# Gate tiles multiplied between the items of an attention, a one-pass decay row and unpaired first tiles, in a fp32-exact transformer kernel on one Trainium2 core

## The reference, cut to what matters

```python
h = _rms_norm(x, g_mix)
fq, fk, fv, f_logit, dq, dk, dv, gate_a, gate_b = split(h @ w_in)
log_f = log_sigmoid(f_logit + b_fgate)
y_a = fox_attention(fq, fk, fv, log_f)       # 8 heads of 64; scores + c_q - c_k, c = cumsum(log_f)
y_b = diff_attention(q1, q2, k1, k2, dv, lam)  # 4 heads, two score maps each, v of width 128
y_b = rms_norm(y_b, g_diff_sub) * (1 - lambda_init)
merged = sigmoid(gate_a) * (y_a @ w_branch_a) + sigmoid(gate_b) * (y_b @ w_branch_b)
x = x + merged @ w_out
x = x + cross_attention(rms_norm(x), rms_norm(mem))
x = x + moe(rms_norm(x))                     # 32 experts, top 2
```

## Time and profile before

| what | us |
|---|---|
| median of three runs | 2947.47 |
| the runs' range | 2941.38 to 2956.33 |
| the profiled execution's own time | 2968.1 |
| its span, first to last instruction | 2966.3 |
| gate tiles of the second block, PE | 1885.6 to 1972.9 |
| attention of the second block, PE | 1973.6 to 2141.1 |
| merge starts, PE | 2149.2 |

### The profile page before, as it was taken

One profiled execution on the slowest core, in us unless ns is written; L12 is line 12 of the kernel. 1 busy time (PEld: TensorE's weight loads), 2 busy tenths in 40 slices (PEclk: granted clock), 3 DMA queues, 4 the chain that ended last, 5 costly groups with the idle time before them and its releaser, 6 DMA issues.

```text
span 2966.3 us, 37460 instructions
## 1 busy us (share of the span) xinstructions
PE 2731.7 (92%) x12718; PEld 2092.8 (71%) x12718; DVE 1462.4 (49%) x2107; ACT 897.8 (30%) x1468; POOL 1151.4 (39%) x768
## 2 busy tenths in 40 slices
PE   6989898999989889999999999999899699999995
PEld 4768777887867777777887777776576466666662
DVE  4673664122345854751213343015655577887785
ACT  3322322111024213311110020112202376776774
POOL 3752015666747720046666645440053011112120
PEclk9999899999999998999999999987999799999997
DMA  3213002332322111012333222320023199999995
GB/s 125 64 36 93 8 15 78 99 93 91 92 71 73 55 44 58 1 58 98 93 98 109 92 69 88 100 64 1 1 78 121 42 359 344 393 390 358 386 393 201
DMA packets 78151, 373.33 MB, mean 126 GB/s; under 512 B 11216, under 2 KB 11344, under 8 KB 53328
## 3 DMA queue, kind: packets, MB, share of 16 engines
q1 hardware_dynamic: 71888, 360.23, 34.5%
q0 software_dynamic: 5280, 8.40, 0.9%
q10 hardware_dynamic: 864, 3.15, 0.3%
HBM read 368.06 MB, written 12.58 MB: 128 GB/s over the span
## 4 chain that ended last, share of the span: by engine, by line
PE 83%; DVE 6%; POOL 3%; issue 3%; ACT 2%; DMA 2%; DVEq 0%; ACTq 0%; SPq 0%; POOLq 0%
PE PS L1807 16%; PE PS L1808 15%; PE PS L1809 15%; PE PS L2169 6%; PE PS L2192 4%; PE PS L2259 4%; PE PS L2260 4%; PE PS L2289 3%; PE PS L1932 2%; PE PS L1829 2%; PE PS L2183 2%; PE PS L2269 2%; PE PS L2129 2%; PE PS L1884 1%; PE PS L2247 1%
## 5 line engine op out<-in xcount | busy, mean ns | idle before, releaser
L565 POOL TENSOR_SCALAR whi<-ring 128x1024 fp32r<-128x1024 f32 x260 | 293.3, 1128 | 1210.2 <-PE PS L1809 963.5
L568 POOL TENSOR_TENSOR wlo<-ring,whi 128x1024 fp32r<-128x1024 f32 x260 | 655.6, 2522 | 21.7
L1807 PE MATMUL PS<-xh,whi 128*128 128x512 f32 x1264 | 504.9, 399 | 30.8 <-POOL wlo L568 24.3
L1808 PE MATMUL PS<-xl,whi 128*128 128x512 f32 x1264 | 496.6, 393 | 0.0
L1809 PE MATMUL PS<-xh,wlo 128*128 128x512 f32 x1264 | 496.5, 393 | 0.0
L1566 DVE TENSOR_TENSOR arena_r<-arena,arena_r 128x1024 fp32r<-128x1024 f32 x256 | 301.6, 1220 | 90.6 <-ACT arena_r L958 87.8
L1807 PEld LDWEIGHTS PS<-xh,whi 128*128 128x128 f32 x1264 | 240.3, 190 | 88.8 <-issue 17.2
L958 ACT ACTIVATE arena_r<-arena 128x1024 fp32r<-128x1024 f32 x256 | 255.9, 1050 | 91.2 <-DMA arena<-w_gate 91.0
L1808 PEld LDWEIGHTS PS<-xl,whi 128*128 128x128 f32 x1264 | 240.6, 190 | 52.2 <-issue 2.9
L1809 PEld LDWEIGHTS PS<-xh,wlo 128*128 128x128 f32 x1264 | 240.1, 190 | 50.9
L1807 PE MATMUL PS<-xs,whi 128*128 128x512 f32 x560 | 231.2, 413 | 17.4 <-DVE xs L1241 10.1
(11 more groups left out here) (390 smaller groups left out, 4494.0 us busy)
## 6 DMA issues: line engine op xcount, KB each, us to landing
ring<-ring_w SPq DMA_DIRECT2D x280, 512.0 KB, 3.5
arena<-w_gate SPq DMA_DIRECT2D x64, 1024.0 KB, 7.6
arena<-w_up SPq DMA_DIRECT2D x64, 1024.0 KB, 9.2
arena<-w_down SPq DMA_DIRECT2D x64, 1024.0 KB
arena<-y_dram SPq DMA_DIRECT2D x8, 512.0 KB, 7.2
xT<-xT_in SPq DMA_DIRECT2D x1, 2048.0 KB, 8.4
out<-arena SPq DMA_DIRECT2D x4, 512.0 KB, 2.6
arena<-memT_in SPq DMA_DIRECT2D x1, 1024.0 KB, 7.5
```

Source lines behind the costliest of these rows:

```text
L565: nc.gpsimd.tensor_scalar(whi[:, t % 2, :], ring[:, t % RING, :], 1.0, 0.0, ALU.mult, ALU.add).then_inc(sems["whi"], 1)
L568: nc.gpsimd.tensor_tensor(wlo[:, t % RING, :], ring[:, t % RING, :], whi[:, t % 2, :], ALU.subtract).then_inc(sems["split"], 1)
L1807: mm(out, a[0], b[0], start=start, stop=False)
L1808: mm(out, a[0], b[1], start=False, stop=False)
```

## The change

1. **Gate tiles.** Feats 18 to 33 leave `STEPS2`. Their 16 tiles are cut into 64 parts of two chunks (six matmuls each) that PE multiplies at the end of the attention's steps: two parts for each of the items 0 to 7, one for each of the items 8 to 55, none for 56 to 63. They accumulate in PSUM bank 2, so the scores of this attention have two banks and item k waits for the exponential of item k - 2. ACT copies a finished tile out without the sigmoid, one step later. The 16 sigmoids stand at the merge.
2. **The attention's results.** Since `xh` and `xl` stay in use for the gates, the results of query blocks 0 to 2 are kept in fp32 where the queries were (`fq`, `dq`), and split by ACT (`xh`) and DVE (`xl`) in eight chunks of 384 columns in the steps of items 60 to 63. The last query block is split as before. The merge waits for all eight.
3. **Decay row.** `negc` is rounded to fp32r in rows 0 to 7 with its rest in rows 64 to 71, and the selector has a 1 in both rows, so that a single fp32r matmul adds both parts. The selector is loaded to `gtmp` ahead of feat 16 and rounded by ACT into `tabs` (`selr`), on which the attention waits.
4. **First tiles.** `first_pair` is gone. The first tile alone waits chunk by chunk: 16 matmuls on `xh`, 8 on `xl`; the second is an ordinary tile. In `late_norm` ACT squares each chunk right behind its rounding, and the sum over the squares stands one tile earlier on PE.

```diff
+        def banks(items):
+
+            return 2 if items is BL2 else 3
+
+        def gate_parts(it):
+
+            k = it.get("k", 64) if it else 64
+            n = 2 * k if k < 8 else 8 + k
+            return range(n, n + 2 if k < 8 else n + 1) if k < 56 else range(0)
+
+        def late_chunks(it):
+
+            k = it.get("k", 0) if it else 0
+            return range(2 * (k - 60), 2 * (k - 60) + 2) if k >= 60 else range(0)
+
+        done = slice(0, (QT - 1) * P)
+        y_mix = [(fq if j < 4 else dq)[:, j % 4, done] for j in range(8)]
+        late_mix = [it["t"] for it in BL2 if it and it["kind"] == "mix"][2 * QT - 3]
 ...
                     nc.scalar.activation(xh[:, c, :], xT[:, c, :], ACT.Identity, scale=lcol[:, C_FFN + c:C_FFN + c + 1]
                                          ).then_inc(sems["xh"], 1)
-                for c in range(KO):
                     nc.scalar.activation(sq8[:, c, :], xT[:, c, :], ACT.Square).then_inc(sems["sq"], 1)
 ...
-                    elif i < 34:
-                        tables["set"] = None
-                        ins = nc.scalar.activation(sga[:, i - 18, :], src, ACT.Sigmoid)
 ...
+                elif kind == "selr":
+                    act_e.wait_ge(sems["sel"], 16)
+                    nc.scalar.activation(sel_r, sel, ACT.Identity).then_inc(sems["selr"], 1)
+                elif kind == "merge":
+                    tables["set"] = None
+                    act_e.wait_ge(sems["evac"], nth("evac", l, 34))
+                    for c in range(8):
+                        for part in (c, 8 + c):
+                            ins = nc.scalar.activation(sga[:, part, :], sga[:, part, :], ACT.Sigmoid)
+                        ins.then_inc(sems["sgs"], 1)
 ...
+            def gate_evac(l, n):
+
+                i = 18 + n // 4
+                act_e.wait_ge(sems["tile"], nth("tile", l, tile2_of(i) + 1))
+                nc.scalar.activation(sga[:, i - 18, :], PS[:, 2, :], ACT.Identity).then_inc(sems["evac"], 1)
 
             def attend(l, items):
                 ln_exp_tables()
                 for s in range(len(items) + 5):
+                    if items is BL2:
+                        for n in gate_parts(items[s - 1] if 0 < s <= len(items) else None):
+                            if n % 4 == 3:
+                                gate_evac(l, n)
+                        for c in late_chunks(items[s] if s < len(items) else None):
+                            if c == 0:
+                                act_e.wait_ge(sems["tile"], nth("tile", l, tile2_of(33) + 1))
+                                act_e.wait_ge(sems["pt"], nth("pt", l, late_mix + 1))
+                            nc.scalar.activation(xh[:, c, done], y_mix[c], ACT.Identity).then_inc(sems["yh"], 1)
 ...
-                    nc.vector.tensor_scalar(negc[0:8, :], qg[0:8, 0, :], -1.0, None, ALU.mult).then_inc(sems["nck"], 1)
+                    nc.vector.tensor_scalar(negc_r[0:8, :], qg[0:8, 0, :], -1.0, None, ALU.mult).then_inc(v_ch, 1)
+                    v.wait_ge(v_ch, v_step())
+                    nc.vector.scalar_tensor_tensor(out=negc_r[64:72, :], in0=qg[0:8, 0, :], scalar=-1.0,
+                                                   in1=negc_r[0:8, :], op0=ALU.mult, op1=ALU.subtract
+                                                   ).then_inc(sems["nck"], 1)
 ...
-                        v.wait_ge(sems["evac"], nth("evac", l, 34))
+                        v.wait_ge(sems["sgs"], c + 1)
 ...
+                                y, late = it["y"], it["mixn"] > 2 * QT - 2
                                 if "sub" in it:
 
-                                    nc.vector.tensor_scalar(gtmp[:, 0:T], PS[:, 3 + t % 2, :], par[:, M_SUB:M_SUB + 1],
-                                                            0.8, ALU.mult, ALU.mult).then_inc(v_ch, 1)
+                                    ins = nc.vector.tensor_scalar(y, src, par[:, M_SUB:M_SUB + 1], 0.8, ALU.mult,
+                                                                  ALU.mult)
+                                    if late:
+                                        ins.then_inc(v_ch, 1)
+                                        v.wait_ge(v_ch, v_step())
+                                elif late:
+                                    y = src
+                                else:
+                                    ins = nc.vector.tensor_copy(y, src)
+                                if late:
+                                    yh, yl = (x[:, it["dst"], it["cols"]] for x in (xh, xl))
+                                    nc.vector.tensor_copy(yh, y).then_inc(v_ch, 1)
                                     v.wait_ge(v_ch, v_step())
-                                    src = gtmp[:, 0:T].rearrange("p (a b) -> p a b", b=P)
-                                nc.vector.tensor_copy(yh, src).then_inc(v_ch, 1)
-                                v.wait_ge(v_ch, v_step())
-                                ins = nc.vector.tensor_tensor(yl, src, yh, ALU.subtract)
+                                    ins = nc.vector.tensor_tensor(yl, y, yh, ALU.subtract)
 ...
+                    for c in late_chunks(items[s]) if items is BL2 and s < len(items) else ():
+                        v.wait_ge(sems["yh"], c + 1)
+                        nc.vector.tensor_tensor(xl[:, c, done], y_mix[c], xh[:, c, done], ALU.subtract
+                                                ).then_inc(sems["yl"], 1)
 ...
-            def feature_major(out, t):
-
+            def feature_major(l, out, t, wait, wait_low=None):
+
+                if wait is None:
+                    for c in range(KO):
+                        ins = mm3(out, weights(t, slice(c * P, c * P + P)), (xh[:, c, :], xl[:, c, :]),
+                                  start=(c == 0), stop=(c == 7))
+                    return ins
                 for c in range(KO):
-                    ins = mm3(out, weights(t, slice(c * P, c * P + P)), (xh[:, c, :], xl[:, c, :]),
-                              start=(c == 0), stop=(c == 7))
+                    pe.wait_ge(sems["xh"], nth("xh", l, wait + c + 1))
+                    for w in weights(t, slice(c * P, c * P + P)):
+                        mm(out, w, xh[:, c, :], start=(c == 0 and w.name == whi.name), stop=False)
+                for c in range(KO):
+                    pe.wait_ge(sems["xn"], nth("xn", l, (wait if wait_low is None else wait_low) + c + 1))
+                    ins = mm(out, whi[:, t % 2, c * P:c * P + P], xl[:, c, :], start=False, stop=(c == 7))
                 return ins
-
-            def first_pair(l, bank, t, high, low):
-
-                for j in range(2):
-                    pe.wait_ge(sems["split"], nth("split", l, t + j + 1))
-                for c in range(KO):
-                    pe.wait_ge(sems["xh"], nth("xh", l, high + max(c, 1) + 1))
-                    for j in range(2):
-                        for w in weights(t + j, slice(c * P, c * P + P)):
-                            mm(PS[:, bank + j, :], w, xh[:, c, :], start=(c == 0 and w.name == whi.name), stop=False)
-                for c in range(KO):
-                    pe.wait_ge(sems["xn"], nth("xn", l, low + c + 1))
-                    for j in range(2):
-                        ins = mm(PS[:, bank + j, :], whi[:, (t + j) % 2, c * P:c * P + P], xl[:, c, :],
-                                 start=False, stop=(c == 7))
-                        if c == 7:
-                            ins.then_inc(sems["tile"], 1)
 ...
-                    first_pair(l, 0, T_FFI, 8, 8)
-                    for u in range(2, 4):
+                    for u in range(4):
                         pe.wait_ge(sems["split"], nth("split", l, T_FFI + u + 1))
-                        feature_major(PS[:, u, :], T_FFI + u).then_inc(sems["tile"], 1)
-                        if u == 2:
+                        feature_major(l, PS[:, u, :], T_FFI + u, 8 if u == 0 else None).then_inc(sems["tile"], 1)
+                        if u == 1:
 ...
-                elif kind == "feat" and i in (0, 34):
-                    pe.wait_ge(sems["evac"], nth("evac", l, i))
-                    first_pair(l, 0, tile2_of(i), *((0, 0) if i == 0 else (8, 16)))
-                elif kind == "feat" and i not in (1, 35):
+                elif kind == "feat":
 ...
-                        ins = feature_major(PS[:, i % 2, :], t)
+                        ins = feature_major(l, PS[:, i % 2, :], t, {0: 0, 34: 8}.get(i), {0: 0, 34: 16}.get(i))
+                    pe.wait_ge(sems["selr"], 1)
+                    pe.wait_ge(sems["yl"], 8)
 ...
+                        nb = banks(items)
+                        if k >= nb:
+                            pe.wait_ge(sems["p"], nth("p", l, k - nb + 1))
 ...
+                    for n in gate_parts(items[s]) if items is BL2 and s < len(items) else ():
+                        gate_part(l, n)
+
+            def gate_part(l, n):
+
+                i, q = 18 + n // 4, n % 4
+                t = tile2_of(i)
+                if q == 0:
```

(12 more changed lines are left out.)

39 lines of the change are left out of this document (18 added, 21 removed).

## The result

| | before | changed |
|---|---|---|
| first comparison, median of 5 runs each | 2947.47 us (2936.41 to 2956.33) | 2920.32 us (2913.41 to 2922.6) |
| ratio, 95% interval | | 0.9887 (0.985 to 0.9923) |
| a second comparison of the same two kernels | 2952.36 us (17 runs) | 2911.16 us (6 runs), ratio 0.9851 (0.9824 to 0.9878) |
| profiled execution | 2968.1 us, span 2966.3 | 2913.41 us, span 2911.6 |

So the change makes the kernel faster, by 27 us in the one comparison and 41 in the other. 2890 was forecast, with 2872 to 2925 as its range. The second comparison comes from the experiments, where the changed kernel ran once more as after_again.

The account below looks back on a forecast made before the run. TensorE was taken to bound the attention, at half clock in its first part, and GpSimd's splits behind norms. Terms -27 - 14 - 2.5 + 5.5 = -38, with -20 for first tiles -58, from median 2947.47 to 2890 us; range 2872 to 2925.

Parts of the forecast that it names:

- 1, the clock, -27: Second block's attention: gate parts between items keep TensorE's clock up through the half-speed stretch, -27 us, bounds 30 and about 10.
- The dip at the start: Start of the attention: one short clock dip while TensorE waits there, counted as 3 us lost.
- The first rival (clock low in part): Attention: the clock stays low in part, so its gain is 10 us or less; 2915 us, chance 0.13.
- the slower one (gate parts run cold): Attention: gate parts do not lift the clock and run at half speed; +18, 2966 us, chance 0.04.
- 2, decay rows, -14: Attention: decay rows in one fp32r pass instead of fp32, -14 us, bounds 16 and 10.5.
- The sign "0.23 to 0.3 us": Attention: a decay row of 512 columns was to take 0.23 to 0.3 us after the change.
- 3 and 4, gaps and costs of the interleaving, +3 together: Attention: gate parts fill TensorE's waits behind combines, -2.5 us; start, junctions and late splits cost +5.5.
- The item on splits: Gate tiles: GpSimd's splits, 3.5 us each, are hidden behind 5.4 us of gate work plus the items.
- The rival of the binding chain: Attention: with two banks TensorE waits for maximum and exponential in narrow items; 2905 us, chance 0.04.
- 5, first tiles, -20: Behind norms: first tiles run alone, so TensorE no longer waits for GpSimd's third-tile split; -20 us, bounds -6 and -26.
- the forecast for the cross attention's pair (+1): Cross attention's start needs both tiles and no third, so unpairing them costs +1 us.
- the second rival: Behind norms: a thin first tile keeps the clock down through the second; first tiles give -4, 2906 us, chance 0.10.

Follow-up runs that it names:

- gates_alone: Kernel before with only gate parts between the attention's items, sigmoids at the merge and two score banks; 2931.41 us, ratio 0.9925.
- fill experiments: Changed kernel plus 37, 15 or 24 dummy multiplications in the cross attention, results unread; 2911.39, 2909.55 and 2909.45 us.
- no_decay: Changed kernel with its decay rows in fp32 again, as before; 2924.95 us, ratio 0.9905.
- shift: Changed kernel with its gate parts two items earlier, so GpSimd's next split no longer falls beside a combine; 2897.37 us, ratio 0.979.
- pairs_back: Changed kernel with the first tiles behind norms paired again; 2936.62 us, ratio 0.9937.
- first_tiles_alone: Kernel before with only the first tiles behind norms unpaired; 2944.56 us, ratio 0.9971.
- before_again: Kernel before, unchanged, run and profiled again; 2952.6 us, ratio 1.0, span 2948.7.
- after: Changed kernel as first measured and profiled, against the kernel before; 2920.32 us, ratio 0.9887.
- decay_only: Kernel before with only the one-pass decay rows; 2978.73 us, ratio 1.0089.
- before: The kernel without the change, as first measured and profiled; 2947.47 us.
- shift_again: Changed kernel with gate parts two items earlier, the same version run once more; 2906.84 us, ratio 0.985.
- fill_burst: Changed kernel plus 24 dummy multiplications in the first three steps of the cross attention; 2909.45 us, ratio 0.9826.
- fill_light: Changed kernel plus 15 dummy multiplications, 4 behind the cross attention's first step and one behind each of the next 11; 2909.55 us, ratio 0.9822.

## Why the prediction was right, and where not

The direction and the range held (2920.32 and 2911.16, in 2872 to 2925), and the mechanism of the main term too. The likeliest value, 2890, is 21 to 30 us too low, and the gain that it stood for, 58 us, came to 27 and 41. By its steps:

- **1, the clock, -27.** Right. The granted clock is 1.00 through the whole attention, in both traces of the change and also where only this part was made (gates_alone). The dip at the start, for which 3 us were counted, did not come, although TensorE waited 2.00 us there. The first rival (clock low in part) did not happen, and the slower one (gate parts run cold) neither. All ten traces with gate parts in this attention have it at 0.97 or more, with 13.7 us at half clock at most; all four without them have 27 to 150 us of it. That dense multiplications are what holds the clock fits this and the fill experiments, which tried it in another stage. Two score banks did not cost the clock: 1.00 over the attention with two, 0.80 with three before.
- **2, decay rows, -14.** Mis-sized: -9.6 by no_decay against the change. A 512-column row is followed at 2036.74 - 2036.40 = 0.34 us, not 0.23; the narrow ones at 0.17 (128 columns), 0.22 and 0.29, where 0.1 had been taken for the narrow sizes. With these numbers the step's own sum is 8 x (0.62 + 0.46 + 0.32 + 0.16) = 12.5. Another 1.9 us went into waits: with the lighter rows TensorE stands idle for 3.7 us in this attention, with the fp32 rows for 1.8. The last 1.0 us to 9.6 is left unexplained. The sign "0.23 to 0.3 us" for a row of 512 columns was missed with 0.34. The change's rows:

```profile
2036.40 0.50 PE L2215 MATMUL PS<-ekb_r,tabs_r 128*128 128x512 f32 x1
2036.74 0.23 PE L2215 MATMUL PS<-maskb 128*128 128x128 bf16 x1
```

- **3 and 4, gaps and costs of the interleaving, +3 together.** For attention and gates -36.4 was measured and -38 forecast, but this agreement is partly luck. The interleaving (items 1, 3 and 4, forecast -24) gave -28.0 in the trace of gates_alone (226.4 us from the end of the key and value tile to the last product, against 254.4), and the decay rows gave 8.4 where 14 was forecast (9.6 less a wait at the start that grew by 1.2 us with their selector). The two errors have opposite signs. Gaps were to give 2.5; instead, the waits for VectorE behind combines are 3.2 + 0.4 us. The item on splits said "Hidden", and asked only whether TensorE waits for them. It did not ask what GpSimd's work does to VectorE's beside it: that is 4 us (shift). The rival of the binding chain did not come: no wait of TensorE in this attention ended with an exponential. The Trainium skill (SBUF — State Buffer, Who interferes with whom) has this rule: GpSimd and a VectorE operation with two inputs in SBUF take turns at one port, whoever comes second waits for the other to end. The trace agrees, with 2.68 us instead of 0.69.
- **5, first tiles, -20.** Right in sum. Up to the attention the parts were -7.9, -7.2 and -4.4, together -19.5, where its items give -7.6, -10.2 and -5; the saving is 17.2 by pairs_back and 17.6 by first_tiles_alone. TensorE no longer waits for GpSimd there; the forecast for the cross attention's pair (+1) was right too (+1.6 from norm to start). That a first tile with few multiplications leaves the second cold was the second rival; it did not come.
- **The sum, -58.** Up to the cross attention -56.2. The step that failed is the one that ended the list there: it took everything behind the changed stages as unchanged, and wrote "+1" for the cross attention's start and nothing for the stage itself. This stage runs the same kind of short fp32 matmuls whose clock the first item was about, and it ran at half clock in both traces of the change: +14.5.
- **The range.** Its ends have two slips: the upper takes 9 us for item 5, whose own bound was 6 (2928 then), and 2947.5 - 74 is 2873.5, not 2872. Neither matters for the result.
- **The median.** Subtracting from the median instead of the profiled time was right, but the reason offered for the 21 us (a shorter stretch at half clock in the timed runs) was wrong: the profiled execution had two waits for a gather, 16.3 us. With what was measured the sum is 2947.5 - 56.2 + 14.5 + 3.4 (the end of the kernel against before_again) = 2909, against medians of 2920.32 and 2911.16.

The parts do not add up. Alone, against 2952 to 2955: gates -21, first tiles -10, decay rows +24; together -27 to -41. The decay rows are the clearest: with the gates they win 9.6 us, without them they lose 24. Whether the other stages of small matmuls run at half clock decides as much as the work that is removed.

**What stays open:** what decides the level of the cross attention. It was cold in after, after_again, first_tiles_alone, no_decay, decay_only and pairs_back, warm in before, before_again, gates_alone, shift and shift_again. Pairing, decay rows and gates each stand on both sides, so none of them decides it alone. Among the versions with unshifted gate parts and no dummies, those with unpaired first tiles or one-pass decay rows were cold and those with neither warm; only shift, which has both, breaks this. What the traces also show is when the stage starts, counted from the start of the last short dip of the clock ahead of it: 12.2 us in before, before_again and gates_alone (warm) and 12.4 in decay_only and pairs_back (cold), 13.5 in both traces of shift (warm) and 13.7 and 13.9 in those of the change (cold), 8.1 in first_tiles_alone and no_decay (cold). So a few tenths of a us in the stage's start may decide the level; no run tests this. Versions that were profiled twice gave the same level both times, which speaks for the version, and the spread of the timed runs speaks for the execution; there is no trace of an execution that would settle it.

## What to carry to other kernels

Where a stage of short, thin matmuls runs at half clock, moving independent dense matmuls between them can pay by the clock, not by filling gaps; take it as a condition for every other saving in that stage, for a part that only removes work there can make it slower. When a change alters or moves the work ahead of a stage of this kind, look up every later one too, and give its level a chance of its own in both directions. And an engine that was idle in a stage is no free cover: ask which port or buffer its neighbours use at the moment that its work is released.

## What the runs showed of the hardware

- TensorE counted as busy for 41.00 of 41 and 44.00 of 44 us at a granted clock of 0.50 (decay_only), and with 24 dense matmuls at the start of a stage, or 15 spread over it, the same small ones ran at 1.00 throughout (fill_burst, fill_light); without them the clock fell to 0.50 3.4 us into the stage (after).
- The cross attention's 134 matmuls take 25.4 us at full clock and 38.9 to 40.9 when all but their first 2 to 5 us are at half clock, a factor of 1.5 to 1.6.
- The same 11 matmuls, 2.3 us busy in 3, opened that stage at clock 1.00 in before and in the change; the clock stayed in the one and fell in the other.
- A VectorE subtraction of 512 fp32 columns with both inputs in SBUF takes 0.69 us, and 2.68 to 2.78 when GpSimd's subtraction of 1024 columns started just ahead of it. GpSimd's takes 2.38 us there, no more than without VectorE beside it (2.38 in shift). Two VectorE products that read PSUM ran beside GpSimd's other operation at their usual 1.29 us together.
- A selector matmul in fp32r with 128, 256, 384 and 512 columns takes 0.17, 0.22, 0.29 and 0.34 us to the next start, so it does not fall to a quarter with a quarter of the columns.
- Two waits of 4.6 us for an indirect gather cost 16.3 us in all, as the clock fell behind each. They come in some executions and not in others of the same kernel.
